# Reordering the seam between the output projection and the feed-forward block of a hybrid encoder layer, on VectorE, ScalarE and GpSimd

## Chip, cores and metric

The kernel runs on one core of one Trainium2 chip. The metric is the device time of one execution in microseconds (us); lower is better. TensorE does the matrix products, VectorE (DVE in the rows), ScalarE (ACT) and GpSimd (POOL) the element-wise work, SyncE (SP) issues the loads.

## The reference, cut to what matters

One layer with D = 1024, 1024 tokens, batch 1, everything in float32. After the mixing part (sliding-window attention beside an mLSTM, outside this change):

```python
mix = jnp.concatenate([rms_norm(att, g_attn_out[l]), rms_norm(mh, g_mlstm_out[l])], axis=-1)
x = x + mix @ w_out[l]
h2 = rms_norm(x, g_ffn[l])
x = x + (jax.nn.silu(h2 @ w_gate[l]) * (h2 @ w_up[l])) @ w_down[l]
```

`w_gate` and `w_up` are 1024 x 2816, `w_down` is 2816 x 1024.

## The kernel before

**Precision and tiles.** Each float32 operand is split into a high part (a copy in a rounded type, made by ScalarE) and a low part (raw minus high, made by VectorE for activations and by GpSimd for weights), and each product is three matmuls: high by high (line 794), high by low (L795 or L796 by the order of operands), low by high. The 1024 tokens are eight tiles of 128 rows, numbered 0 to 7. A transposed activation lies as 128 x 4 x 128 pieces, four k-slices of one tile; four such tiles make a 128 x 2048 array.

**Seven forms.** The feed-forward products use a 2x2 block scheme with seven products in place of eight. The activations are cut into quarters (tiles 0 to 3 or 4 to 7, first or second half of D), the weights of 256 columns likewise, and each of the seven products, called forms and done in the order `FORMS = (1, 2, 6, 5, 7, 3, 4)`, multiplies a quarter or a sum of quarters by a weight quarter or a sum of them. `hf_raw[f]`, `hf_hi[f]` and `hf_lo[f]` are the activation side of form f, `wr_raw`, `wr_hi`, `wr_lo` the weight side. For each activation tile 4 to 7, VectorE's `form_tile` makes four sums at L1640: form 5 from 7 and 4, form 7 from 6 and 7, form 6 from 5 and 6, form 3 from 3 and 6 (each name being the array that holds the operand; the sums overwrite it). For each weight block GpSimd makes four sums (`block_sum`, L724, forms 5, 6, 7, 4) and seven low parts (`block_low`, L730). A sum waits until TensorE has finished with the slot's last use, and until the loads it needs have landed; a low part waits for ScalarE's high copy (`weight_high`, L1288), and that one for the sum.

**Products and their order.** One `half_product` is 12 matmuls of 128 x 512. A block q is one gate or one up block of 256 feed-forward columns, seven products: q = 0 the first gate, q = 1 the first up block, q = 2 the second gate. P1 to P14 are the fourteen products of q = 0 and 1 (`first_gate_up`, L1094), interleaved:

```text
P1 gate form 1     P2 up form 1     P3 gate form 2    P4 up form 2
P5 gate form 6     P6 gate form 5   P7 gate form 7    P8 gate form 3    P9 gate form 4
P10 up form 6      P11 up form 5    P12 up form 7     P13 up form 3     P14 up form 4
```

Products 15 to 21 are the second gate (`gate_up`), product 21 its form 4. Tile 7 is transposed on TensorE (L814) inside P2. The results are combined outside TensorE: ScalarE copies one product from PSUM to `sg[..]` (gate) or `af_raw[..]` (up) with `copy_product`, VectorE adds another one to it with `add_product` (L1968). `sg[1]`, `sg[4]`, `sg[2]` are such partial results of the gate; ScalarE takes the SiLU of them, and VectorE multiplies by the up part (`gated`, L1971). P9 writes into the bank whose earlier content (P7's result) the addition to `sg[4]` reads, so P9 waits for that addition (`added`, second of the block) and for the sixth low part of the activations; product 21 waits for the addition to `sg[4]` of its block in the same way:

```python
pe.wait_ge(added, add_of(0, 1))
pe.wait_ge(h2_flo, 6)
half_product(gate, 0, 4, False)
```

**The seam.** The output projection runs as 16 steps j = 0 to 15, j // 8 choosing the half of the columns, j % 8 the tile. At each step VectorE adds two PSUM banks to the residual x, the first residual addition at L1874 (after `wa_done`) and the second at L1878 (after `wb_done`). From j = 8 on, with tile s = j - 8 then complete, ScalarE takes its statistics (L1472, then `rstd`), VectorE normalises it into `h2buf` (L1660), TensorE transposes it at the next step, ScalarE copies the transposed tile out (`form_tile` of ScalarE), and VectorE makes the sums of a tile two steps behind: tile 4 in step j = 14, tile 5 in j = 15, both after the second residual addition and ahead of the normalisation; tiles 6 and 7 in `dve_first`. After that, VectorE works down a list written by hand (`dve_first`, L2028): the low parts of form 6 (L1652, three quarters, then one), the addition to `sg[1]`, low part 5, the addition to `af_raw[1]`, low parts 7, 3 and 4, one `gated`, the addition to `sg[4]`, and so on. ScalarE's list is `act_first` (L1546), and GpSimd's is the loop over q (L733).

**After P14** VectorE's list goes on with `act_sums` and `dve_gate` of the second gate: `gated` (L1971), four sums (L1982 to 1987), one `act_low` (L1992, the low parts `af_lo` of the up part), one addition, six more `act_low`, and then the addition to `sg[4]` that product 21 waits for. All later gates have the same list. The down block that follows every pair adds PSUM to x on VectorE (L2068).

Of the kernel before, what the change touches and what calls it, by code (L numbers as in the profile page):

```python
# [35 lines left out]
P = 128  # L36
# [38 lines left out]
def hymba_block(nc, x, g_mix, w_in, b_gates, conv_qk, q_gain, k_gain, sinks,  # L75
# [31 lines left out]
    with ctx:  # L107
# [353 lines left out]
        def sum_count(q, f):  # L461

            if q >= QA:
                return 4 * QA + LAST_SUMS.index((q, f)) + 1
            return 4 * q + {5: 1, 6: 2, 7: 3, 4: 4}[f]
# [186 lines left out]
        def _(pool):  # L652
# [80 lines left out]
            for q in range(QA):  # L733
                n = 16 * (q // 2 + 1)
                if q == 1:
# [5 lines left out]
                    block_sum(q, 5, 7, 5)  # L741
                else:
# [5 lines left out]
                pool.wait_ge(wsum, 4 * q + 1)  # L748
                pool.wait_ge(b22_s[q % 2], n)
                block_sum(q, 6, 3, 5)  # L750
                pool.wait_ge(wsum, 4 * q + 2)
                block_sum(q, 7, 3, 7)
                if q == 1:
                    pool.wait_ge(b21_again, 16)
                    block_sum(q, 4, 4, 6)
                else:
# [4 lines left out]
                pool.wait_ge(wsum, 4 * q + 4)  # L761
                for f in FORMS[2:]:
                    block_low(q, f)
# [27 lines left out]
        def _(pe):  # L791
# [302 lines left out]
            def first_gate_up():  # L1094
# [9 lines left out]
                pe.wait_ge(h2_flo, 2)  # L1104
                half_product(gate, 0, 6, False)
                pe.wait_ge(wa_free, 2 * T)
                pe.wait_ge(h2_flo, 3)
                half_product(gate_f, 0, 5, True)
                pe.wait_ge(copied, copy_of(0, 1))
                pe.wait_ge(h2_flo, 4)  # L1110
                half_product(gate, 0, 7, False)
                pe.wait_ge(copied, copy_of(0, 2))
                pe.wait_ge(h2_flo, 5)
                half_product(gate_f, 0, 3, False)
                pe.wait_ge(added, add_of(0, 1))
                pe.wait_ge(h2_flo, 6)
# [107 lines left out]
        def _(act):  # L1224
# [135 lines left out]
            for U in range(ALL):  # L1360
# [105 lines left out]
                if s >= 0:  # L1466
# [79 lines left out]
            def act_first():  # L1546
# [4 lines left out]
                form_high(6, slice(0, 3 * P))  # L1551
# [50 lines left out]
        def _(dve):  # L1602
# [24 lines left out]
            def form_tile(t):  # L1627

                a = slice(t % 4 * P, (t % 4 + 1) * P)
                if t < 4:  # L1630
                    for b in range(2):
                        dve.wait_ge(h2_raw, 2 * t + b + 1)
                        V_.tensor_tensor(hf_lo[1 + b][:, :, a], bank[2 + b][:, :].rearrange("p (k n) -> p k n", k=4),
                                         hf_hi[1 + b][:, :, a].bitcast(F32), ALU.subtract).then_inc(h2_split, 1)
                    return
                dve.wait_ge(h2_raw, 2 * t + 2)
                n = 4 * (t - 4)

# [58 lines left out]
            for U in range(ALL):  # L1697
# [261 lines left out]
                if s >= 6:  # L1959
                    form_tile(s - 2)  # L1960
# [159 lines left out]
```

## Time and profile before

| quantity | value |
|---|---|
| median of 3 runs | 1032.83 us (1032.19 to 1033.6) |
| the profiled execution | 1031.43 us |
| its span | 1029.6 us |
| TensorE matmul busy | 1014.2 us, 99% |
| TensorE weight loads busy | 834.8 us, 81% |
| VectorE busy | 668.5 us, 65% |
| ScalarE busy | 431.9 us, 42% |
| GpSimd busy | 688.9 us, 67% |
| mean granted TensorE clock | 0.997 |
| HBM read, written | 60.48 MB, 4.21 MB |

The profiled execution takes 1.8 us more than its span: that is what lies around the recorded instructions. Its time is 1.40 us under the median of the runs and 0.76 under the quickest of them. Busy shares are means over the whole program; weight loads overlap matmuls. The granted clock is given as a share of full speed, so 1.00 is the 2.4 GHz level. Times within the trace are counted from the start of the span. The step j = 13 of the seam lies at 370 us, P1 starts near 387, P14 ends near 429, and product 21 runs at 446.

### The profile page before, as it was taken

What the parts mean: (1) busy time and instruction counts of PE and PEld (TensorE: products, weight loads), DVE (VectorE), ACT (ScalarE), POOL (GpSimd) and SP (SyncE); (2) the same over time, 40 slices, a digit from 0 to 9 for tenths busy, and PEclk for the clock granted to TensorE, in tenths of its full rate; (3) what the DMA queues carried; (4) which work ended last, traced back from release to release, by engine and by line L of the source; (5) the groups of instructions that cost most, each with busy time, mean ns of one, the idle gap of its engine ahead of it and who ended that gap; (6) DMA issues with size and microseconds to landing.
All of it is one profiled execution on the core that took longest, in us unless ns stands there. A gap on an engine that the chain in (4) does not pass through costs nothing.

```text
span 1029.6 us, 13475 instructions
## 1 busy us (share of the span) xinstructions
PE 1014.2 (99%) x4970; PEld 834.8 (81%) x4970; DVE 668.5 (65%) x790; ACT 431.9 (42%) x895; POOL 688.9 (67%) x543
## 2 busy tenths in 40 slices
PE   9999999999989999999999999999999999999998
PEld 7898778887878887888888888888888888888887
DVE  4259449867772569474857677574857677574585
ACT  7545133347750457533434242433434243433440
POOL 0138668826566514977778688688778688688792
PEclk9999999999999999999999999999999999999999
DMA  7223212140021002111211211211211211211213
GB/s 234 60 62 82 82 33 71 48 147 22 32 104 60 22 21 82 41 52 42 82 41 42 82 42 42 81 41 41 82 42 42 82 41 42 82 41 42 76 62 139
DMA packets 71162, 66.06 MB, mean 64 GB/s; under 512 B 5305, under 2 KB 53689, under 8 KB 71097
## 3 DMA queue, kind: packets, MB, share of 16 engines
q1 hardware_dynamic: 70104, 64.71, 20.3%
q8 instruction: 40, 0.66, 0.3%
q10 hardware_dynamic: 992, 0.49, 0.2%
q14 instruction: 26, 0.20, 0.1%
HBM read 60.48 MB, written 4.21 MB: 63 GB/s over the span
## 4 chain that ended last, share of the span: by engine, by line
PE 75%; DVE 17%; issue 4%; ACT 2%; POOL 1%; DMA 0%; SPq 0%; DVEq 0%; POOLq 0%
PE banks L794 23%; PE banks L796 23%; PE banks L795 23%; DVE af_lo L1992 7%; DVE af_raw L1982 1%; DVE af_raw L1984 1%; ACT prob L1458 1%; PE banks L814 1%; DVE sg L1968 1%; DVE af_raw L1971 1%; PE banks L880 1%; DVE hf_lo L1652 1%; DVE prob L1910 1%; DVE af_raw L1987 1%; DVE smx L1915 1%
## 5 line engine op out<-in xcount | busy, mean ns | idle before, releaser
L730 POOL TENSOR_TENSOR wr_lo<-wr_raw,wr_hi 128x512 fp32r<-128x512 f32 x231 | 316.9, 1401 | 26.9 <-ACT wr_hi L1288 21.8
L724 POOL TENSOR_TENSOR wr_raw<-wr_raw,wr_raw 128x512 f32<-128x512 f32 x132 | 193.0, 1466 | 145.5 <-PE banks L796 113.0
L794 PE MATMUL banks<-hf_hi,wr_hi 128*128 128x512 f32 x616 | 242.4, 394 | 2.8 <-DVE sg L1968 2.0
L796 PE MATMUL banks<-hf_hi,wr_lo 128*128 128x512 f32 x616 | 241.1, 391 | 0.0
L795 PE MATMUL banks<-hf_lo,wr_hi 128*128 128x512 f32 x616 | 240.7, 391 | 0.0
L2068 DVE TENSOR_TENSOR x<-banks,x 128x1024 f32<-128x1024 f32 x138 | 168.8, 1224 | 56.9 <-PE banks L796 43.0
L1288 ACT ACTIVATE wr_hi<-wr_raw 128x512 fp32r<-128x512 f32 x231 | 136.5, 625 | 157.1 <-POOL wr_raw L724 97.6
L794 PE MATMUL banks<-w_hi,actT_hi 128*128 128x512 f32 (+1 forms) x448 | 172.7, 385 | 0.9 <-DVE w_lo L1665 0.9
L796 PE MATMUL banks<-w_hi,actT_lo 128*128 128x512 f32 (+1 forms) x448 | 168.5, 376 | 0.0
L795 PE MATMUL banks<-w_lo,actT_hi 128*128 128x512 f32 (+1 forms) x448 | 168.5, 376 | 0.0
L794 PEld LDWEIGHTS banks<-hf_hi,wr_hi 128*128 128x128 f32 x616 | 116.0, 188 | 31.7 <-DVE sg L1968 6.8
L796 PEld LDWEIGHTS banks<-hf_hi,wr_lo 128*128 128x128 f32 x616 | 115.9, 188 | 25.0
L795 PEld LDWEIGHTS banks<-hf_lo,wr_hi 128*128 128x128 f32 x616 | 116.1, 188 | 24.5
L794 PE MATMUL banks<-wr_hi,af_hi 128*128 128x512 f32 x308 | 120.4, 391 | 0.0
L795 PE MATMUL banks<-wr_lo,af_hi 128*128 128x512 f32 x308 | 120.3, 391 | 0.0
L796 PE MATMUL banks<-wr_hi,af_lo 128*128 128x512 f32 x300 | 117.2, 391 | 0.0
L1968 DVE TENSOR_TENSOR af_raw<-banks,af_raw 128x512 f32<-128x512 f32 x33 | 22.8, 691 | 134.5 <-PE banks L796 134.5
L666 POOL TENSOR_TENSOR w_lo<-w_raw,w_hi 128x512 fp32r<-128x512 f32 (+1 forms) x48 | 61.0, 1271 | 70.5 <-ACT w_raw L1304 67.9
L794 PEld LDWEIGHTS banks<-w_hi,actT_hi 128*128 128x128 f32 x448 | 84.5, 189 | 17.5 <-issue 2.1
L796 PEld LDWEIGHTS banks<-w_hi,actT_lo 128*128 128x128 f32 x448 | 84.6, 189 | 15.7
L795 PEld LDWEIGHTS banks<-w_lo,actT_hi 128*128 128x128 f32 x448 | 84.7, 189 | 13.8
L1992 DVE TENSOR_TENSOR af_lo<-af_raw,af_hi 128x512 fp32r<-128x512 f32 x75 | 90.8, 1263 | 0.3
(202 smaller groups left out, 1210.9 us busy)
## 6 DMA issues: line engine op xcount, KB each, us to landing
wr_raw<-in_w_up SPq DMA_DIRECT2D x46, 256.0 KB, 3.3
wr_raw<-in_w_gate SPq DMA_DIRECT2D x44, 256.0 KB, 3.4
wr_raw<-in_w_down SPq DMA_DIRECT2D x44, 256.0 KB, 3.0
w_raw<-in_w_in SPq DMA_DIRECT2D x32, 256.0 KB, 3.5
w_raw<-in_w_out SPq DMA_DIRECT2D x16, 256.0 KB, 2.6
x<-in_x SPq DMA_DIRECT2D x8, 512.0 KB, 6.4
out<-x SPq DMA_DIRECT2D x16, 256.0 KB, 2.2
x_in<-in_x SPq DMA_DIRECT2D x7, 512.0 KB, 4.4
```

Of the source, the lines that this page charges most:

```text
L666: nc.gpsimd.tensor_tensor(w_lo[:, ring, 0:width], w, w_hi[:, ring, 0:width].bitcast(F32), ALU.subtract).then_inc(w_ready, 1)
L724: nc.gpsimd.tensor_tensor(wr_raw[slot(q, f)][:, :], wr_raw[slot(q, a)][:, :], wr_raw[slot(q, b)][:, :], ALU.subtract).then_inc(wsum, 1)
L730: nc.gpsimd.tensor_tensor(wr_lo[s][:, :], wr_raw[s][:, :], wr_hi[s][:, :].bitcast(F32), ALU.subtract).then_inc(wf_lo, 1)
L794: nc.tensor.matmul(ps, x_hi, wh, start=first, stop=False, skip_group_check=more)
L795: nc.tensor.matmul(ps, x_hi, wl, start=False, stop=False, skip_group_check=more)
L796: return nc.tensor.matmul(ps, x_lo, wh, start=False, stop=last, skip_group_check=more)
L814: last = nc.tensor.transpose(bank[2 + b][:, j * P:(j + 1) * P], src[t % len(src)][:, (4 * b + j) * P:(4 * b + j + 1) * P], ident[:, :])
L880: last = nc.tensor.matmul(bank[6 + i][:, region], scd[:, 2 * pair + i, :], mvx[:, t, 2 * pair + i, :], start=True, stop=t == 0)
L1288: nc.scalar.activation(wr_hi[s][:, :], wr_raw[s][:, :], ACT.Copy).then_inc(wf_hi, 1)
L1968: V_.tensor_tensor(dst[:, :], src[:, :], dst[:, :], ALU.add).then_inc(added, 1)
L1992: V_.tensor_tensor(af_lo[b][f][:, :], af_raw[b][f][:, :], af_hi[b][f][:, :].bitcast(F32), ALU.subtract).then_inc(act_lo_s, 1)
L2068: V_.tensor_tensor(xs, banks[first + h][:, :, :], xs, ALU.add).then_inc(down_add, 1)
```

## The change

Four edits, all between 376 and 425 us of the program:

1. **Sums.** VectorE's `form_tile` for tiles 4 to 7 is cut in two, `first_sums` (forms 5 and 7) and `last_sums` (forms 6 and 3). For tiles 4 and 5 the first two now run between the two residual additions of j = 14 and 15; the last two stay where all four were.
2. **Form 6's first quarter.** The high copy (ScalarE) and the low part (VectorE) of tile 4's quarter of form 6 are made in the seam, the low part in j = 15 between the residual additions; the later instruction covers two quarters in place of three. The counts of `h2_flo` that TensorE waits for go up by one.
3. **`sg[4]`.** ScalarE's copy of P6 to `sg[4]` comes ahead of the SiLU of `sg[1]`, and VectorE's addition to it ahead of low part 4 and of one `gated`.
4. **GpSimd's order for the first up block (q = 1).** Sums 5, 6, 4, low parts 6 and 5, sum 7, low parts 7, 3, 4, in place of sums 5, 6, 7, 4 and low parts 6, 5, 7, 3, 4. The other gate and up blocks keep their order.

The diff, cut to these (the counts of `h2_flo` in `first_gate_up` rise from 2, 3, 4, 5, 6 to 3, 4, 5, 6, 7 in the same way as shown once):

```diff
@@ sum_count
+            if q == 1:
+                return 4 * q + {5: 1, 6: 2, 4: 3, 7: 4}[f]
             return 4 * q + {5: 1, 6: 2, 7: 3, 4: 4}[f]
@@ GpSimd, q == 1
                     block_sum(q, 5, 7, 5)
+                    pool.wait_ge(wsum, sum_count(q, 5))
+                    pool.wait_ge(b22_s[q % 2], n)
+                    block_sum(q, 6, 3, 5)
+                    pool.wait_ge(b21_again, 16)
+                    pool.wait_ge(wsum, sum_count(q, 6))
+                    block_sum(q, 4, 4, 6)
+                    pool.wait_ge(wsum, sum_count(q, 4))
+                    block_low(q, 6)
+                    block_low(q, 5)
+                    block_sum(q, 7, 3, 7)
+                    pool.wait_ge(wsum, sum_count(q, 7))
+                    for f in FORMS[4:]:
+                        block_low(q, f)
...
-                if q == 1:
-                    pool.wait_ge(b21_again, 16)
-                    block_sum(q, 4, 4, 6)
@@ first_gate_up
                 pe.wait_ge(added, add_of(0, 1))
-                pe.wait_ge(h2_flo, 6)
+                pe.wait_ge(h2_flo, 7)
                 half_product(gate, 0, 4, False)
@@ ScalarE, after form_tile(s - 1)
+                    if s == 6:
+                        act.wait_ge(wb_done, T + 5)
+                        act.wait_ge(h2_sum, 3)
+                        form_high(6, slice(0, P))
@@ act_first
-                form_high(6, slice(0, 3 * P))
+                form_high(6, slice(P, 3 * P))
...
                 form_high(4, slice(0, 4 * P))
+                copy_product(sg[4], bank[0], product(0, 5))
                 act.wait_ge(added, add_of(0, 0))
                 silu_of(sg[1], sg[1])
-                copy_product(sg[4], bank[0], product(0, 5))
@@ VectorE
+            def first_sums(t):
+
                 dve.wait_ge(h2_raw, 2 * t + 2)
+                combine(t, 5, 7, 4, ALU.add)
+                combine(t, 7, 6, 7, ALU.subtract)
+
+            def last_sums(t):
+
                 n = 4 * (t - 4)
...
                 dve.wait_ge(h2_sum, n + 2)
+                combine(t, 6, 5, 6, ALU.subtract)
                 dve.wait_ge(h2_sum, n + 3)
+                combine(t, 3, 3, 6, ALU.subtract)
@@ between the residual additions
+                    if j >= T + 6:
+                        first_sums(j - T - 2)
+                    if j == T + 7:
+                        dve.wait_ge(h2_sum, 4)
+                        form_low(6, slice(0, P), 1)
@@ after the second residual addition
                 if s >= 6:
-                    form_tile(s - 2)
+                    last_sums(s - 2)
@@ dve_first
-                form_low(7, slice(0, 4 * P), 4)
-                form_low(3, slice(0, 4 * P), 5)
-                form_low(4, slice(0, 4 * P), 6)
+                form_low(7, slice(0, 4 * P), 5)
+                form_low(3, slice(0, 4 * P), 6)
+                dve.wait_ge(copied, copy_of(0, 2))
+                add_product(sg[4], bank[4], product(0, 7))
+                form_low(4, slice(0, 4 * P), 7)
                 dve.wait_ge(silu_done, 1)
                 dve.wait_ge(added, add_of(1, 0))
                 gated(0, 0, 1, af_raw[0][1])
-                dve.wait_ge(copied, copy_of(0, 2))
-                add_product(sg[4], bank[4], product(0, 7))
```

How the orders on the engines move, at three places (each row is line, operation, output and inputs, shape).

VectorE at j = 15, before. `x_109` is the residual, `hf_raw_149`, `152`, `146`, `155`, `158` are forms 5, 7, 6, 3, 4, `h2buf_114` the normalised tile.

```order
L1874 SCALAR_TENSOR_TENSOR x_109<-banks,rmix,x_109 128x512
L1878 SCALAR_TENSOR_TENSOR x_109<-banks,rmix,x_109 128x512
L1640 TENSOR_TENSOR hf_raw_149<-hf_raw_152,hf_raw_158 128x4x128
L1640 TENSOR_TENSOR hf_raw_152<-hf_raw_146,hf_raw_152 128x4x128
L1640 TENSOR_TENSOR hf_raw_146<-hf_raw_149,hf_raw_146 128x4x128
L1640 TENSOR_TENSOR hf_raw_155<-hf_raw_155,hf_raw_146 128x4x128
L1660 SCALAR_TENSOR_TENSOR h2buf_114<-x_109,rstd,g_row 128x1024
```

and in the change, where `hf_lo_145` is form 6's low part:

```order
L1892 SCALAR_TENSOR_TENSOR x_109<-banks,rmix,x_109 128x512
L1651 TENSOR_TENSOR hf_raw_149<-hf_raw_152,hf_raw_158 128x4x128
L1651 TENSOR_TENSOR hf_raw_152<-hf_raw_146,hf_raw_152 128x4x128
L1670 TENSOR_TENSOR hf_lo_145<-hf_raw_146,hf_hi_144 128x4x128
L1901 SCALAR_TENSOR_TENSOR x_109<-banks,rmix,x_109 128x512
L1651 TENSOR_TENSOR hf_raw_146<-hf_raw_149,hf_raw_146 128x4x128
L1651 TENSOR_TENSOR hf_raw_155<-hf_raw_155,hf_raw_146 128x4x128
L1678 SCALAR_TENSOR_TENSOR h2buf_114<-x_109,rstd,g_row 128x1024
```

Two of the four sums and the new quarter of form 6 now stand ahead of the second residual addition.

VectorE in `dve_first`, behind form 5's low part, before. `hf_lo_151`, `154`, `157` are low parts 7, 3, 4; `sg_254` is `sg[4]`, `sg_252` `sg[1]`, `sg_253` `sg[2]`, `af_raw_212` the up part that is first gated.

```order
L1968 TENSOR_TENSOR af_raw_212<-banks,af_raw_212 128x512
L1652 TENSOR_TENSOR hf_lo_151<-hf_raw_152,hf_hi_150 128x2048
L1652 TENSOR_TENSOR hf_lo_154<-hf_raw_155,hf_hi_153 128x2048
L1652 TENSOR_TENSOR hf_lo_157<-hf_raw_158,hf_hi_156 128x2048
L1971 TENSOR_TENSOR af_raw_212<-af_raw_212,sg_252 128x512
L1968 TENSOR_TENSOR sg_254<-banks,sg_254 128x512
L1968 TENSOR_TENSOR sg_253<-banks,sg_253 128x512
```

and in the change:

```order
L1991 TENSOR_TENSOR af_raw_212<-banks,af_raw_212 128x512
L1670 TENSOR_TENSOR hf_lo_151<-hf_raw_152,hf_hi_150 128x2048
L1670 TENSOR_TENSOR hf_lo_154<-hf_raw_155,hf_hi_153 128x2048
L1991 TENSOR_TENSOR sg_254<-banks,sg_254 128x512
L1670 TENSOR_TENSOR hf_lo_157<-hf_raw_158,hf_hi_156 128x2048
L1994 TENSOR_TENSOR af_raw_212<-af_raw_212,sg_252 128x512
L1991 TENSOR_TENSOR sg_253<-banks,sg_253 128x512
```

The addition to `sg[4]` moved from behind the low part of form 4 and the gated product to ahead of both.

GpSimd in the first up block, before. `wr_raw_161`, `167`, `164`, `176` are the sums of forms 5, 6, 7, 4; `wr_lo_166`, `160`, `163`, `178`, `175` the low parts of forms 6, 5, 7, 3, 4.

```order
L724 TENSOR_TENSOR wr_raw_161<-wr_raw_164,wr_raw_161 128x512
L724 TENSOR_TENSOR wr_raw_167<-wr_raw_179,wr_raw_161 128x512
L724 TENSOR_TENSOR wr_raw_164<-wr_raw_179,wr_raw_164 128x512
L724 TENSOR_TENSOR wr_raw_176<-wr_raw_176,wr_raw_167 128x512
L730 TENSOR_TENSOR wr_lo_166<-wr_raw_167,wr_hi_165 128x512
L730 TENSOR_TENSOR wr_lo_160<-wr_raw_161,wr_hi_159 128x512
L730 TENSOR_TENSOR wr_lo_163<-wr_raw_164,wr_hi_162 128x512
L730 TENSOR_TENSOR wr_lo_178<-wr_raw_179,wr_hi_177 128x512
L730 TENSOR_TENSOR wr_lo_175<-wr_raw_176,wr_hi_174 128x512
```

and in the change:

```order
L726 TENSOR_TENSOR wr_raw_161<-wr_raw_164,wr_raw_161 128x512
L726 TENSOR_TENSOR wr_raw_167<-wr_raw_179,wr_raw_161 128x512
L726 TENSOR_TENSOR wr_raw_176<-wr_raw_176,wr_raw_167 128x512
L732 TENSOR_TENSOR wr_lo_166<-wr_raw_167,wr_hi_165 128x512
L732 TENSOR_TENSOR wr_lo_160<-wr_raw_161,wr_hi_159 128x512
L726 TENSOR_TENSOR wr_raw_164<-wr_raw_179,wr_raw_164 128x512
L732 TENSOR_TENSOR wr_lo_163<-wr_raw_164,wr_hi_162 128x512
L732 TENSOR_TENSOR wr_lo_178<-wr_raw_179,wr_hi_177 128x512
L732 TENSOR_TENSOR wr_lo_175<-wr_raw_176,wr_hi_174 128x512
```

Sum 7 moved behind the low parts of forms 6 and 5.

## Rows read from the trace of the kernel before

**Rows 1.** The page's busy time of each engine.

```profile
PE 1014.2 (99%) x4970; PEld 834.8 (81%) x4970; DVE 668.5 (65%) x790; ACT 431.9 (42%) x895; POOL 688.9 (67%) x543
```

**Rows 2.** List of TensorE's waits: engine, line, releaser, total, times, longest.

```profile
PE banks L794 <- DVE sg L1968: 2.0, 1, 2.0
```

**Rows 3.** TensorE's timeline: start, length, line, instruction, idle before with releaser.

```profile
389.51 0.73 PE L814 MATMUL banks<-ident,h2buf 128*128 128x128 f32 x5
...
402.57 0.39 PE L796 MATMUL banks<-hf_hi,wr_lo 128*128 128x512 f32 x1
403.14 0.47 PE L794 MATMUL banks<-hf_hi,wr_hi 128*128 128x512 f32 x1 [0.18 <-issue]
...
408.48 0.39 PE L796 MATMUL banks<-hf_hi,wr_lo 128*128 128x512 f32 x1
410.87 0.50 PE L794 MATMUL banks<-hf_hi,wr_hi 128*128 128x512 f32 x1 [2.00 <-DVE sg L1968]
...
445.71 0.39 PE L794 MATMUL banks<-hf_hi,wr_hi 128*128 128x512 f32 x1
```

**Rows 4.** TensorE after two earlier gaps, then stretches (PEclk: granted clock).

```profile
233.79 1.16 PE L949 MATMUL banks<-ident,prob 128*128 128x128 f32 x8 [1.94 <-POOL prob L689]
...
304.29 0.87 PE L949 MATMUL banks<-ident,prob 128*128 128x128 f32 x6 [1.88 <-POOL prob L689]
...
234.00:238.00 4.00, 4.00 (x16) 3.35 (x15) 3.86 (x8) 1.18 (x5) 3.05 (x3) 0.59 0.00 0
304.00:308.00 4.00, 3.71 (x33) 3.27 (x34) 1.22 (x3) 2.00 (x5) 3.84 (x5) 1.00 0.00 0
412.00:416.00 4.00, 4.00 (x12) 3.11 (x11) 0.00 (x0) 2.25 (x6) 4.00 (x4) 0.57 0.00 0
416.00:420.00 4.00, 4.00 (x19) 3.21 (x18) 0.00 (x0) 1.55 (x3) 3.92 (x4) 1.00 0.02 4
```

**Rows 5.** VectorE's timeline, the residual additions of j = 13 to 15.

```profile
374.57 1.29 DVE L1660 SCALAR_TENSOR_TENSOR h2buf<-x,rstd,g_row 128x1024 f32<-128x1024 f32 x1 [1.78 <-ACT rstd L1239]
...
378.40 0.75 DVE L1878 SCALAR_TENSOR_TENSOR x<-banks,rmix,x 128x512 f32<-128x512 f32 x1 [1.88 <-PE banks L796]
...
384.75 0.75 DVE L1878 SCALAR_TENSOR_TENSOR x<-banks,rmix,x 128x512 f32<-128x512 f32 x1 [1.08 <-PE banks L796]
...
388.07 1.28 DVE L1660 SCALAR_TENSOR_TENSOR h2buf<-x,rstd,g_row 128x1024 f32<-128x1024 f32 x1
```

**Rows 6.** GpSimd's timeline, seam and second gate.

```profile
376.11 2.54 POOL L730 TENSOR_TENSOR wr_lo<-wr_raw,wr_hi 128x512 fp32r<-128x512 f32 x2 [10.45 <-ACT wr_hi L1288]
...
403.60 7.75 POOL L724 TENSOR_TENSOR wr_raw<-wr_raw,wr_raw 128x512 f32<-128x512 f32 x3 [2.71 <-PE banks L796]
411.43 6.28 POOL L730 TENSOR_TENSOR wr_lo<-wr_raw,wr_hi 128x512 fp32r<-128x512 f32 x5
...
435.08 1.62 POOL L724 TENSOR_TENSOR wr_raw<-wr_raw,wr_raw 128x512 f32<-128x512 f32 x1 [1.42 <-PE banks L796]
...
440.60 4.26 POOL L724 TENSOR_TENSOR wr_raw<-wr_raw,wr_raw 128x512 f32<-128x512 f32 x3 [2.20 <-PE banks L796]
```

**Rows 7.** One line's instructions, 485 to 504 us: shortest, median, longest in ns.

```profile
L1992 DVE TENSOR_TENSOR af_lo<-af_raw,af_hi x7: 681/1772/1786, 493.4 to 500.9; 128x512 fp32r<-128x512 f32 x7
```

**Rows 8.** ScalarE's timeline, the statistics of j = 15.

```profile
385.53 1.06 ACT L1472 ACTIVATE h2buf<-x 128x1024 f32<-128x1024 f32 x1 [3.66 <-DVE x L1878]
```

**Rows 9.** VectorE's timeline, the low parts of forms 7, 3 and 4.

```profile
400.25 8.28 DVE L1652 TENSOR_TENSOR hf_lo<-hf_raw,hf_hi 128x2048 fp32r<-128x2048 f32 x3
```

**Rows 10.** VectorE's timeline, the chain after a block's last product.

```profile
429.34 0.69 DVE L1971 TENSOR_TENSOR af_raw<-banks,sg 128x512 f32<-128x512 f32 x1 [0.27 <-PE banks L796]
...
443.25 0.69 DVE L1968 TENSOR_TENSOR sg<-banks,sg 128x512 f32<-128x512 f32 x1 [0.80 <-PE banks L796]
...
486.92 0.69 DVE L1971 TENSOR_TENSOR af_raw<-banks,sg 128x512 f32<-128x512 f32 x1 [0.55 <-PE banks L796]
...
494.59 8.09 DVE L1992 TENSOR_TENSOR af_lo<-af_raw,af_hi 128x512 fp32r<-128x512 f32 x6
```

More of the change, by code:

```diff
@@ L747, in _ @@
                     block_low(q, 1)
[L748 to L752, printed above, removed]
-                if q == 1:
-                    pool.wait_ge(b21_again, 16)
-                    block_sum(q, 4, 4, 6)
-                else:
+                    pool.wait_ge(wsum, 4 * q + 1)
+                    pool.wait_ge(b22_s[q % 2], n)
+                    block_sum(q, 6, 3, 5)
+                    pool.wait_ge(wsum, 4 * q + 2)
+                    block_sum(q, 7, 3, 7)
                     pool.wait_ge(b21_s[q % 2], n)
@@ L760, in _ @@
                     block_low(q, 2)
-                pool.wait_ge(wsum, 4 * q + 4)
-                for f in FORMS[2:]:
-                    block_low(q, f)
+                    for f in FORMS[2:]:
+                        block_low(q, f)
             for q in (QA, QB):
@@ L1629, in form_tile, with combine @@
                 a = slice(t % 4 * P, (t % 4 + 1) * P)
[L1630 to L1635, printed above, removed]
+                for b in range(2):
+                    dve.wait_ge(h2_raw, 2 * t + b + 1)
+                    V_.tensor_tensor(hf_lo[1 + b][:, :, a], bank[2 + b][:, :].rearrange("p (k n) -> p k n", k=4),
+                                     hf_hi[1 + b][:, :, a].bitcast(F32), ALU.subtract).then_inc(h2_split, 1)
+            def combine(t, f, x, y, op):
+                a = slice(t % 4 * P, (t % 4 + 1) * P)
+                V_.tensor_tensor(hf_raw[f][:, :, a], hf_raw[x][:, :, a], hf_raw[y][:, :, a],
+                                 op).then_inc(h2_sum, 1)
+            def first_sums(t):
                 dve.wait_ge(h2_raw, 2 * t + 2)
+                combine(t, 5, 7, 4, ALU.add)
+                combine(t, 7, 6, 7, ALU.subtract)
+            def last_sums(t):
                 n = 4 * (t - 4)
-                def combine(f, x, y, op):
-                    V_.tensor_tensor(hf_raw[f][:, :, a], hf_raw[x][:, :, a], hf_raw[y][:, :, a],
-                                     op).then_inc(h2_sum, 1)
-                combine(5, 7, 4, ALU.add)
-                combine(7, 6, 7, ALU.subtract)
                 dve.wait_ge(h2_sum, n + 2)
-                combine(6, 5, 6, ALU.subtract)
+                combine(t, 6, 5, 6, ALU.subtract)
                 dve.wait_ge(h2_sum, n + 3)
-                combine(3, 3, 6, ALU.subtract)
+                combine(t, 3, 3, 6, ALU.subtract)
             def form_low(f, a, count):
@@ L2028, in dve_first @@
             def dve_first():
-                form_tile(T - 2)
-                form_tile(T - 1)
+                for t in (T - 2, T - 1):
+                    first_sums(t)
+                    last_sums(t)
                 dve.wait_ge(h2_sum, 12)
-                form_low(6, slice(0, 3 * P), 1)
+                form_low(6, slice(P, 3 * P), 2)
                 dve.wait_ge(h2_sum, 16)
-                form_low(6, slice(3 * P, 4 * P), 2)
+                form_low(6, slice(3 * P, 4 * P), 3)
                 dve.wait_ge(copied, copy_of(0, 0))
                 add_product(sg[1], bank[5], product(0, 2))
-                form_low(5, slice(0, 4 * P), 3)
+                form_low(5, slice(0, 4 * P), 4)
                 dve.wait_ge(copied, copy_of(1, 0))
                 add_product(af_raw[0][1], bank[6], product(1, 2))
-                form_low(7, slice(0, 4 * P), 4)
-                form_low(3, slice(0, 4 * P), 5)
-                form_low(4, slice(0, 4 * P), 6)
+                form_low(7, slice(0, 4 * P), 5)
[3 more added lines that the diff above has]
+                form_low(4, slice(0, 4 * P), 7)
                 dve.wait_ge(silu_done, 1)
```

8 lines of the change are left out of this document (4 added, 4 removed).

## The prediction

> **What bounds the kernel now.** I read four views: busy time, TensorE's waits, the timelines of the four engines at the seam, and the table of stretches with TensorE's clock. TensorE is busy 99% of the span [rows 1], so the end is set by its idle gaps and by its clock. The longest wait for VectorE in the whole program is 2.0 us for the addition to `sg` [rows 2]. Its place is P9, the gate's fourth-form product: the last matmul of P8 starts at 408.48, the next one should follow 0.23 later, but starts at 410.87, so P9 is 2.16 late [rows 3]. P7 starts at 403.14, 0.34 after its turn. After the long gap the clock falls to the lower level: from 412 to 416 us 12 matmuls start, where 19 do in the next 4 us, so seven matmuls of 0.23, **1.6 us**, are lost. The same happened after a gap of 1.94 us ahead of 233.79 (0.59 of full clock); a gap of 1.88 ahead of 304.29 left it at 1.00 in the 4 us that followed [rows 4]. So P9 costs 3.8 us in this execution, and the question is what part of it comes back.
>
> **The seam's sums (j = 14 and 15).** On VectorE the second residual addition of j = 14 starts at 378.40 after 1.88 idle, so the first one ended at 376.52 [rows 5]. Two sums (0.68 each, the next starting 0.08 before the end, so steps of 0.60) fit into that on paper. But GpSimd runs two low parts there, 376.11 to 378.65 [rows 6]. VectorE's instructions with two SBUF inputs and GpSimd's take turns: of seven `af_lo` the quickest took 0.68 and the typical one 1.77 [rows 7], and three sums of GpSimd beside VectorE's low parts took 7.75, where two instructions alone take 2.54 [rows 6]. So the first sum waits to 377.4, the second to 379.1, and the second residual addition starts at 379.6 instead of 378.4. ScalarE's statistics and the normalisation follow it by 1.78 after its end [rows 5]: normalisation at 382.1 (was 381.73). Then addition 383.3, two sums and the early quarter of form 6 (three times 0.60), second addition **385.8 instead of 384.75**, normalisation 388.35 to 389.6 instead of 388.07 to 389.35. TensorE wants it for tile 7's transposes at 389.51 [rows 3]: 0.1 to 0.2 late, a cost of **0.15**. The early quarter on ScalarE costs nothing: it waits there 3.66 us for the addition [rows 8], and without that cover it would be one copy of 0.6.
>
> **From tile 7 to P9.** The chain of sums starts 0.3 later, and form 6's low part is a quarter (0.6) shorter: form 5's low part starts some 0.3 earlier, 397.2. Form 7's low part waits for GpSimd's sum as before and ends at 402.8 (the row at 400.25 less 0.1) [rows 9], so P7 starts at about 402.95 instead of 403.14. Form 3's low part ends at 405.0. Now comes the moved addition to `sg4`: it needs P7, whose result is there 3.0 after its start, at 405.95. VectorE is idle for 0.9 and adds until 406.65. Meanwhile GpSimd, which waited behind form 3's low part for its sum 6, ends that at 406.2, and its next one is now sum 4, whose weights land about 3.3 after P6 (as sum 6 started 3.36 after P5: 403.60 [rows 6], and P5 ends 2.72, twelve matmuls, before P6's 402.96 [rows 3]), at 406.3. It takes the turn 0.3 us ahead of VectorE's form 4, which therefore runs 407.6 to **409.8** (three low parts of 128x2048 took 8.28 with GpSimd's turns, 0.55 and 1.15, in them, so 2.2 each [rows 9]). P8 ends its turn at 408.6, so P9 waits 1.3 and starts at 409.9: **0.95 earlier**. A gap of 1.3 is below the 1.88 that left the clock alone [rows 4], so the 1.6 comes back too. The ScalarE copy of `sg4` moves ahead of the table load and SiLU (1.9 us) and is then 2.5 us early; the next SiLU waits for the addition to `sg4` in any case, so nothing is queued up there. Together TensorE is **2.55 us ahead** by P10: P14 ends at 426.6 instead of 429.2.
>
> **What GpSimd does meanwhile.** Sum 4 to 407.6; low part 6 behind VectorE's form 4, to 411.0; low part 5 behind the gated product, to 412.7; sum 7 to 414.0. ScalarE's high copy of form 7 can only start then (it could at 411.4, right behind the SiLU, before), and behind it stand form 3, two SiLUs, form 4 and the next gate's weights; the copy that P12 needs ends some 4.3 later, 418.3, against P12's turn at 418.2: 0 to 0.2. Low parts 7, 3, 4 (1.25 each): 414.7 to 418.4, where they ended at 417.7 [rows 6]. P10 to P14 get their low parts in time by 1.5 us or more. But GpSimd is now 0.7 later and TensorE 2.55 earlier: **3.2 us of lead are gone**. Before, GpSimd ran its work for the second gate to 433.7 and then was idle 1.42 and again 2.20 until TensorE's products freed slots (435.08 and 440.60) [rows 6]. Both idle times vanish.
>
> **The second gate.** After P14 VectorE works through 11 instructions with two SBUF inputs (four sums and seven `af_lo`) and one addition, and only then makes the addition that product 21 needs. Free of GpSimd that is 0.7 + 11 x 0.60 + 0.6 = 8 us, and each that is blocked adds 1.77 - 0.68 = 1.1 [rows 7]. Now it takes 429.34 to 442.45, 13.1 us, so between four and five are blocked, since GpSimd is idle in part of it; the addition then still waits 0.8 for TensorE [rows 10]. In the gate of j = 2 it takes 15.7 (486.92 to 502.6), seven blocked, four of them in a row in the last six. With GpSimd never idle all eleven are: 20.1. One or two will slip through, since GpSimd still has waits between a sum and the next: I take **19**, nearest to the full one. Starting 426.8 the addition is at 445.8, and product 21 starts at 446.5; TensorE wants it at 443.1 (six products of 2.75 after P14). So there is a **new stall of 3.4 us**, and product 21 starts 0.8 later than the 445.71 of now [rows 3]. The bounds: 15.7 gives no stall (product 21 at 443.3, 2.4 earlier), 20.1 gives 1.9 later. The Trainium skill (SBUF — State Buffer, Who interferes with whom) has the two kinds of instruction exclude each other for their whole length, whichever was issued first; a pair would then take 0.68 + 1.29 = 1.97, the chain of eleven 23, and product 21 would start near 450. The rows show 1.77 for one that had to wait [rows 7], so the sum goes by that.
>
> After a gap of 3.4, longer than both that brought the lower clock, I take another 1.6. **Sum:** +0.8 +1.6 = +2.4 us. Behind it GpSimd catches up in the down block, where VectorE's additions read PSUM and block nobody, and all later gates stay as they are. The profiled execution took 1031.43 (span 1029.6); by it the changed kernel would take 1033.8. The median of the runs is 1.4 higher, about one stretch of lower clock; I add the change to the median: **1035.2 us**. What a measurement of this kernel can tell from no change is 0.2%, 2.07 us.
>
> **Rivals.** A, the forecast: lead of GpSimd lost, stall at product 21, clock lost there: 1035.2. For it: the second gate has only 0.8 us of slack now, and both idle times of GpSimd lie in it. Against: it rests on taking turns eleven times in a row, of which the rows show four [rows 10].
> B, the stall comes but not the lower clock: +0.8, 1033.6. For it: the gap of 1.88 at 304.3 was spared.
> C, the other side: **the gain is kept.** VectorE's chain after P14 stays at the 15.7 of the later gates, because GpSimd finds its slots or ScalarE's copies not ready often enough. It decides at a chain of 18.2: below that product 21 is earlier than now. Price: 2.4 earlier, 1030.4. For it: the gate of j = 2 runs so, and no later wait of TensorE for VectorE is in the list [rows 2]. Against: there GpSimd is idle part of the chain, as four unblocked instructions show, and here it is behind.
> D, VectorE gets form 4 in ahead of sum 4 (0.3 us decide): P9 at 409.0, but product 21 still hangs on the chain after P14, 0.9 earlier with it: +1.5, 1034.3.
> E, all eleven blocked and the transposes or P12 later than I have it: +3.7, 1036.5.
>
> **Numbers.** A 0.42, B 0.20, C 0.18, D 0.10, E 0.10. Slower by over 0.2% (above 1034.9): most of A, E and a little of D, 0.50. Within 0.2%: B, the rest of A and D, a part of C, 0.34. Faster: C, 0.16. The range leaves out C's better part and a tail of E: 1031.4 to 1036.6.
>
> **What would show it.** P9 starting near 409.9 with 1.3 idle before it and a clock of 1.00 at 412 to 416; VectorE idle ahead of the addition to `sg4`; the second residual addition near 379.6; no idle time of GpSimd between 419 and 441; seven `af_lo` of the second gate nearly all at 1.7; a TensorE wait of 3 us for VectorE at product 21, and a stretch of lower clock behind it. I am wrong if product 21 starts before 445, or if P9's gap stays above 1.9.

## The result, and the profile after

The changed kernel takes **1036.55 us** in the median of 6 runs (1035.5 to 1037.41), the kernel before 1032.31 in 6 runs beside it: a ratio of 1.0038 with a 95% interval of 1.0028 to 1.0048 (the medians themselves lie 4.24 us apart). It is slower, as forecast, and the time lies 0.05 us inside the upper end of the stated range. The profiled execution took 1037.41, with a span of 1035.6; its granted clock is 0.997, as before. It is the slowest of its six, and the profiled one of before was quicker than any of its six, so the two traces lie 6.0 us apart where the medians lie 4.2.

From the page, the busy time of each engine, which answers to [rows 1]:

```profile
PE 1014.8 (98%) x4970; PEld 835.1 (81%) x4970; DVE 676.4 (65%) x791; ACT 431.5 (42%) x896; POOL 691.1 (67%) x543
```

TensorE is as busy as before to 0.6 us, and VectorE is 7.9 us busier with one instruction more: nearly all of that is time in which its instructions wait for GpSimd while they count as busy.

The list of TensorE's waits, which answers to [rows 2]:

```profile
PE banks L804 <- DVE sg L1991: 4.5, 2, 3.2
```

One wait of 2.0 for the addition to `sg` has become two, 3.2 and 1.3. TensorE's timeline has them at these places, with P9 (first row) and product 21 (second); the third row is the same product of the sixth gate (j = 5), 234 us later:

```profile
412.05 0.47 PE L804 MATMUL banks<-hf_hi,wr_hi 128*128 128x512 f32 x1 [1.21 <-issue]
...
448.62 0.50 PE L804 MATMUL banks<-hf_hi,wr_hi 128*128 128x512 f32 x1 [3.17 <-DVE sg L1991]
...
682.44 0.50 PE L804 MATMUL banks<-hf_hi,wr_hi 128*128 128x512 f32 x1 [1.30 <-DVE sg L1991]
```

The table of stretches (columns as in [rows 4]: PE, weight loads, VectorE, ScalarE, GpSimd, then the granted clock), behind P9 and behind product 21:

```profile
414.00:418.00 4.00, 4.00 (x19) 3.23 (x18) 0.24 (x1) 1.91 (x4) 3.19 (x3) 1.00 0.00 0
...
450.00:454.00 4.00, 4.00 (x12) 3.18 (x11) 0.00 (x0) 2.13 (x5) 4.00 (x4) 0.60 0.00 0
```

The clock stays at its upper level behind P9, and the lower level with its 12 matmuls in 4 us, seen at 412 before [rows 4], now stands behind product 21.

VectorE's timeline, the split sums of j = 14 and the chain behind P14, which answer to [rows 5] and [rows 10]:

```profile
377.99 0.75 DVE L1892 SCALAR_TENSOR_TENSOR x<-banks,rmix,x 128x512 f32<-128x512 f32 x1
378.65 3.20 DVE L1651 TENSOR_TENSOR hf_raw<-hf_raw,hf_raw 128x512 f32<-128x512 f32 x2
381.77 0.74 DVE L1901 SCALAR_TENSOR_TENSOR x<-banks,rmix,x 128x512 f32<-128x512 f32 x1
...
408.23 0.69 DVE L1991 TENSOR_TENSOR sg<-banks,sg 128x512 f32<-128x512 f32 x1 [1.09 <-PE banks L806]
408.84 3.11 DVE L1670 TENSOR_TENSOR hf_lo<-hf_raw,hf_hi 128x2048 fp32r<-128x2048 f32 x1
...
428.93 0.69 DVE L1994 TENSOR_TENSOR af_raw<-banks,sg 128x512 f32<-128x512 f32 x1 [0.89 <-PE banks L806]
...
436.13 1.67 DVE L2015 TENSOR_TENSOR af_lo<-af_raw,af_hi 128x512 fp32r<-128x512 f32 x1
437.72 0.68 DVE L1991 TENSOR_TENSOR sg<-banks,sg 128x512 f32<-128x512 f32 x1
438.32 9.64 DVE L2015 TENSOR_TENSOR af_lo<-af_raw,af_hi 128x512 fp32r<-128x512 f32 x6
447.89 1.27 DVE L1991 TENSOR_TENSOR sg<-banks,sg 128x512 f32<-128x512 f32 x2
```

The chain from `gated` to the addition that product 21 waits for takes 447.89 - 428.93 = **18.96 us**; it was 13.1 [rows 10], and 19 was forecast. Its seven `af_lo` average 1.67 us. All eleven of its two-input instructions waited for GpSimd, nine in full (1.67 to 1.78) and two in part (1.34 and 1.18). GpSimd's timeline over the same stretch, to hold against [rows 6]:

```profile
423.24 4.26 POOL L726 TENSOR_TENSOR wr_raw<-wr_raw,wr_raw 128x512 f32<-128x512 f32 x3
427.58 9.68 POOL L732 TENSOR_TENSOR wr_lo<-wr_raw,wr_hi 128x512 fp32r<-128x512 f32 x6
437.21 1.75 POOL L726 TENSOR_TENSOR wr_raw<-wr_raw,wr_raw 128x512 f32<-128x512 f32 x1
439.04 1.62 POOL L732 TENSOR_TENSOR wr_lo<-wr_raw,wr_hi 128x512 fp32r<-128x512 f32 x1
440.61 5.14 POOL L726 TENSOR_TENSOR wr_raw<-wr_raw,wr_raw 128x512 f32<-128x512 f32 x3
```

The idle times of 1.42 and 2.20 are gone: each row begins within 0.1 us of the end of the last one.

**Where the time went.** Take the start of each TensorE matmul in the one trace minus its start in the other, instruction by instruction, and read how this difference moves (plus is slower):

| place | change of the difference, us |
|---|---|
| everything up to 389 us | +2.22 |
| tile 7's transposes | +0.20 |
| P7 | -0.40 |
| P9 | -0.83 |
| lower clock of before, behind P9 | -1.56 |
| product 21 | +3.42 |
| lower clock behind product 21 | +1.59 |
| sixth gate | +1.29 |
| all the rest | +0.09 |

The first row is in code that the change does not touch: start-up (1.36 by 9 us) and a stretch of lower clock that lay behind the gap at 232 us before and lies behind the gap at 303 us here. In the eleven profiles below this row is +0.69 to +1.66, so it is mostly the trace of before that was early. The six rows from the transposes to product 21 and its clock sum to **+2.42 us**; the forecast for them was +2.4. With the first row taken off, product 21 starts at 446.40, where 446.5 was forecast. The sixth gate was not forecast.

### The profile page after: what moved, and what is told of

The parts are those of the page before. It is cut to its first block, busy times and chain, and to the rows that moved or that the text cites. A ratio compares the mean times of both kernels' runs of the same rounds, so it can differ in the third digit from the quotient of the medians.

```text
span 1035.6 us, 13449 instructions
## 1 busy us (share of the span) xinstructions
PE 1014.8 (98%) x4970; PEld 835.1 (81%) x4970; DVE 676.4 (65%) x791; ACT 431.5 (42%) x896; POOL 691.1 (67%) x543
## 3 DMA queue, kind: packets, MB, share of 16 engines
q1 hardware_dynamic: 70104, 64.71, 20.1%
## 4 chain that ended last, share of the span: by engine, by line
PE 73%; DVE 18%; issue 4%; ACT 3%; POOL 1%; DMA 1%; SPq 0%; DVEq 0%; POOLq 0%
PE banks L804 23%; PE banks L806 23%; PE banks L805 22%; DVE af_lo L2015 8%; ACT prob L1468 2%; DVE af_raw L2007 2%; DVE af_raw L2005 2%; PE banks L824 1%; DVE sg L1991 1%; DVE af_raw L2010 1%; PE banks L890 1%; DVE prob L1933 1%; DVE smx L1938 1%; DVE af_raw L1994 1%; PE banks L896 1%
## 5 line engine op out<-in xcount | busy, mean ns | idle before, releaser
L732 POOL TENSOR_TENSOR wr_lo<-wr_raw,wr_hi 128x512 fp32r<-128x512 f32 x231 | 321.6, 1421 | 27.8 <-ACT wr_hi L1298 22.7
L726 POOL TENSOR_TENSOR wr_raw<-wr_raw,wr_raw 128x512 f32<-128x512 f32 x132 | 190.5, 1447 | 146.4 <-PE banks L806 111.4
L804 PEld LDWEIGHTS banks<-w_hi,actT_hi 128*128 128x128 f32 x448 | 84.5, 189 | 18.9 <-DVE w_lo L1683 2.3
L2015 DVE TENSOR_TENSOR af_lo<-af_raw,af_hi 128x512 fp32r<-128x512 f32 x75 | 96.1, 1334 | 0.3
```

What stands on the lines that cost most here:

```text
L726: nc.gpsimd.tensor_tensor(wr_raw[slot(q, f)][:, :], wr_raw[slot(q, a)][:, :], wr_raw[slot(q, b)][:, :], ALU.subtract).then_inc(wsum, 1)
L732: nc.gpsimd.tensor_tensor(wr_lo[s][:, :], wr_raw[s][:, :], wr_hi[s][:, :].bitcast(F32), ALU.subtract).then_inc(wf_lo, 1)
L804: nc.tensor.matmul(ps, x_hi, wh, start=first, stop=False, skip_group_check=more)
L2015: V_.tensor_tensor(af_lo[b][f][:, :], af_raw[b][f][:, :], af_hi[b][f][:, :].bitcast(F32), ALU.subtract).then_inc(act_lo_s, 1)
```

## The experiments

Theory: by P10 TensorE is ahead, GpSimd is not, so GpSimd is never idle in the second gate, blocks VectorE's chain, and product 21 waits. First each part of the change alone. The kernel before, measured beside the runs, had a median of 1032.43 us for the first four, 1032.42 for the next four and 1032.08 for the last three; "quicker than the changed kernel" sets a run's median against 1036.55.

**Edits 1 and 2 alone** (the split sums and the early quarter; GpSimd's order, the copy and the addition to `sg[4]` as before).

> The kernel before with the split sums and the early first quarter of form 6 alone (edits 1 and 2); addition to sg[4] and GpSimd's order as before. Theory (GpSimd loses its lead over TensorE at the second gate): TensorE gains only the 0.1 to 0.3 us by which form 5's low part starts earlier, GpSimd keeps both idle times, no wait at product 21; 0.3 us quicker than before, within 0.5 either way. Rival (the sums between the residual additions delay the tiles): most of the 4.2 us of the whole change are here already, the transposes of tile 7 late by over 1 us.

Measured: 1032.22 us in 11 runs against 1032.43 (26 runs), ratio 0.9998 (0.999 to 1.0007). TensorE's difference to before moves by +0.20 at the transposes, -0.41 at P7 and -0.11 at P9. GpSimd keeps both idle times in the second gate (1.47 and 2.24), and product 21 has no gap. The rival falls: these edits cost nothing to be seen.

**Edit 3 alone.**

```diff
                 form_high(4, slice(0, 4 * P))
+                copy_product(sg[4], bank[0], product(0, 5))
                 act.wait_ge(added, add_of(0, 0))
                 silu_of(sg[1], sg[1])
-                copy_product(sg[4], bank[0], product(0, 5))
...
+                dve.wait_ge(copied, copy_of(0, 2))
+                add_product(sg[4], bank[4], product(0, 7))
                 form_low(4, slice(0, 4 * P), 6)
```

> The kernel before with the earlier copy and addition to sg[4] alone (edit 3). Theory: the gap before P9 falls from 2.0 to about 1.2 us, TensorE is then 0.8 us earlier (2.4 with the clock), GpSimd is not, and product 21 waits 2 to 4 us for VectorE; 2 to 3.5 us slower than before. Rival (the moved addition is a gain that something else in the change gives back): 1 to 2.5 us quicker.

Measured: 1034.59 us, ratio 1.0026 (1.0015 to 1.0036), 2.2 slower by the medians, as expected; the rival falls. P9 is 0.86 earlier. The list of TensorE's waits shows the 2.0 gone and this in its place, at product 21:

```profile
PE banks L794 <- DVE sg L1968: 2.5, 1, 2.5
```

The forecast mechanism appears with this edit by itself, GpSimd's order untouched.

**Edit 4 alone** (GpSimd's new order for the first up block).

> The kernel before with GpSimd's new order for the first up block alone (edit 4). Theory: the gap before P9 stays at 2.0; GpSimd ends the up block's work about 0.7 to 2 us later, VectorE's chain after P14 grows, and product 21 waits 1 to 3 us; 1 to 3 us slower. Rival (the order costs nothing, since GpSimd has 3.6 us of idle time in the second gate): within 0.5 of before.

Measured: 1037.34 us, ratio 1.0046 (1.0029 to 1.0063). P9 waits 2.03 as before. Three waits for `sg` in all:

```profile
PE banks L804 <- DVE sg L1978: 6.1, 3, 2.8
```

2.8 is product 21, 1.3 the sixth gate. GpSimd ends its work for the up block 0.75 later against TensorE, as in the whole change; of its idle times 0.68 and 0.50 are left. So a loss of 0.75 is enough: VectorE's chain takes 18.6 with this edit alone, 18.3 with edit 3 alone, which gives away some 2.3 of lead, and 18.96 with both. The losses do not add, since with either one nearly every instruction of the chain already waits. The miss is in size, 4.9 against 1 to 3: behind product 21 comes the lower clock (1.5), and the sixth gate's 1.3. The seven runs lie in two groups, 1033.2 and 1033.5, and five from 1036.9 to 1039.6; which of the gaps the two quick ones do without, their times do not tell.

**The change without edit 4.**

> The changed kernel with GpSimd's order of before (edits 1 to 3). Theory: lead is lost through TensorE's gain at P9 all the same, and the stall at product 21 stays at 3 to 4 us; 2 to 4 us slower than before. Rival (the order alone makes GpSimd late): product 21 no longer waits and the kernel is 2 us quicker than before.

Measured: 1034.41 us, ratio 1.0022 (1.0013 to 1.003). The wait at product 21 is 2.5 instead of 3.2 (3 to 4 were expected), so edit 4 is the last 0.7 of it, the figure that the prediction had for GpSimd's later end. The rival falls. In this profile no lower clock follows the 2.5; it is the quickest of the eleven runs (1033.03), and what the others had there was not traced.

**VectorE's addition two `af_lo` earlier in the second gate**, in the changed kernel:

```diff
+                late = 2 if j == 1 else 0
                 if j >= 1:
-                    for f in FORMS[1:]:
+                    for f in FORMS[1:len(FORMS) - late]:
                         act_low(j - 1, f)
                 dve.wait_ge(copied, 3 * g + 3)
                 add_product(sg[4], bank[4], 7 * g + 5)
+                if j >= 1:
+                    for f in FORMS[len(FORMS) - late:]:
+                        act_low(j - 1, f)
```

> The changed kernel, but in the second gate VectorE makes the addition to sg[4] two af_lo earlier (ahead of forms 3 and 4, which the down block needs last). Theory (product 21 waits only because the addition stands behind a chain that GpSimd blocks): two blocked af_lo are 3.4 us, the stall of 3.2 us and the lower clock behind it go, and product 21 starts within 0.3 of its turn; 4 to 5 us quicker than the changed kernel, about 1031.5, a little less than before. The af_lo of forms 3 and 4 are made 0.6 later and nobody waits. Rival (TensorE is held by something else at that place, and the wait moves to the down block): over 1034.

Measured: 1031.94 us, 4.6 less than the changed kernel; ratio to before 0.9992 (0.9984 to 1.0001). TensorE's difference moves by 0.12 at product 21, instead of 3.42. The rival falls. The wait at product 21 is worth 4.6 us with what follows it. The sixth gate's gap of 1.3 is still there.

**GpSimd held back**, in the changed kernel: ahead of its first sum for the next block it waits for product 19.

```diff
+                    if q == 3:
+                        pool.wait_ge(gu_done, 19)
                     pool.wait_ge(b11_s[q % 2], n)
```

> The changed kernel, but GpSimd starts its work for the down block that follows the second gate (its sum 5) only when product 19 is done, which gives it back an idle stretch in VectorE's chain. Nothing else moves. Theory: from about 437 us on VectorE's remaining af_lo run unblocked, 0.6 each, and the stall at product 21 falls from 3.2 us to under 0.5; 4 to 5 us quicker than the changed kernel, about 1032. Rival (the chain is slow by itself, GpSimd or not): the stall stays at 3 us, no gain, and GpSimd's delay may add to it.

Measured: 1032.12 us, ratio to before 0.9996 (0.9987 to 1.0005), 4.4 less than the changed kernel. VectorE's chain:

```profile
437.51 3.69 DVE L2017 TENSOR_TENSOR af_lo<-af_raw,af_hi 128x512 fp32r<-128x512 f32 x6
441.93 0.69 DVE L1993 TENSOR_TENSOR sg<-banks,sg 128x512 f32<-128x512 f32 x1 [0.73 <-PE banks L808]
```

and GpSimd's timeline, idle meanwhile:

```profile
426.74 9.70 POOL L732 TENSOR_TENSOR wr_lo<-wr_raw,wr_hi 128x512 fp32r<-128x512 f32 x6
441.91 1.30 POOL L726 TENSOR_TENSOR wr_raw<-wr_raw,wr_raw 128x512 f32<-128x512 f32 x1 [5.47 <-PE banks L808]
```

The same six `af_lo` that took 9.64 take 3.69 once GpSimd is idle. VectorE's list is that of the changed kernel, instruction for instruction: GpSimd is what made it slow. Making an engine wait longer made the kernel 4 us quicker. The delay costs 0.4 us elsewhere, a short gap of TensorE in the down block at 450 us, and the gap of 1.3 us that the sixth gate had stands in the eleventh here.

**GpSimd's work doubled at one place**, in the kernel before.

```diff
+                    if q == 1 and f == 4:
+                        s = slot(q, f)
+                        pool.wait_ge(wf_hi, high_count(q, f))
+                        for n_, op in ((1, ALU.subtract), (2, ALU.add)):
+                            nc.gpsimd.tensor_tensor(wr_raw[s][:, :], wr_raw[s][:, :], wr_hi[s][:, :].bitcast(F32),
+                                                    op).then_inc(again, 1)
+                            pool.wait_ge(again, n_)
                     block_low(q, f)
```

> The kernel before, and GpSimd does two more operations of 128x512 in the first up block (form 4's raw weights minus their high copy, plus it again: the value stays), 2.6 us of its time; TensorE's part up to P14 is untouched. Theory: GpSimd comes 2.6 to 3.4 us later to the second gate, its two idle times there go, four more of VectorE's instructions are blocked, and product 21 waits 2 to 3.5 us, with the lower clock behind it: 3 to 5 us slower than before. Rival (only TensorE being earlier makes the stall, GpSimd's 3.6 us of idle time can take this): within 0.5 of before.

Measured: 1036.47 us, ratio 1.0039 (1.0026 to 1.0051). P9 waits 2.01 as before, product 21 waits 3.1 in the list of waits, the lower clock behind it, and the chain takes 18.9. The rival falls. 2.67 us of GpSimd's time, laid where nobody waits for it, cost 4 us thirty microseconds later.

**The addition one `af_lo` earlier in every gate from the second on**, in the kernel before (`late = 1 if j >= 1 else 0` in the diff above).

> The kernel before, and in every gate from the second on VectorE makes the addition to sg[4] one af_lo earlier (ahead of form 4's). Theory: in each of the nine later gates TensorE waits 0.23 us for it now; with the addition up to 1.7 earlier these go, nine times 0.23 is 2.0 us; 1.5 to 2.1 quicker than before. Rival (the 0.23 is what TensorE takes at a wait of any kind): no change.

Measured: 1028.2 us, ratio **0.9956** (0.9944 to 0.9968), twice the gain expected. In the kernel before the first matmul of a later gate's form 4 stands like this in TensorE's timeline:

```profile
502.88 0.39 PE L796 MATMUL banks<-hf_hi,wr_lo 128*128 128x512 f32 x1
503.34 0.50 PE L794 MATMUL banks<-hf_hi,wr_hi 128*128 128x512 f32 x1
503.68 0.40 PE L795 MATMUL banks<-hf_lo,wr_hi 128*128 128x512 f32 x1
```

0.23 late, and then the matmul after it starts 0.34 behind instead of 0.23. The gap of 0.23 costs 0.36 per gate by the difference of the traces, 3.3 us over the nine gates from the third on (the second has no such gap). The remaining 0.9 of the median's gain is not explained: up to P9 this kernel is the one of before, with the same wait of 2.0 and the same chance of the lower clock behind it.

**All together.** The addition two `af_lo` earlier in the second gate and one in the later ones, in the changed kernel, in that without edit 4, and in a kernel before with edit 3's copy and the addition to `sg[4]` behind form 4's low part but ahead of the gated product.

> The changed kernel, with the addition to sg[4] two af_lo earlier in the second gate and one earlier in every later gate. Theory: the second gate's stall goes as when only that gate was edited, and each of the eight later gates gives the 0.36 us per period that the same edit gave the kernel before (57.73 to 57.37): 2.9 us, with the gates' sensitivity to GpSimd's phase (the 1.3 us gap that single gates showed) gone too; about 1028.5, and 0 to 1 us quicker than the kernel before with that edit alone if the 0.8 us at P9 is kept. Rival (edits do not add: the change still costs something behind the second gate): over 1030.

> As the run above, with GpSimd's order of the kernel before. Theory: GpSimd's order matters only by its 0.7 us of lead; with VectorE's addition early enough both orders are within 0.7 us of each other, about 1028.5. Rival (the new order is what lets TensorE keep the gain): this one is over 1 us slower than the run above.

> The kernel before with the smallest edits: the copy to sg[4] early, the addition to it ahead of the gated product but behind form 4's low part, and the addition in the later gates as in the two runs above. Theory: the gap before P9 falls to about 0.5 us (the gated product, 1.7 blocked, no longer stands in front), of which up to 0.7 comes back before P10; 1 to 1.5 us quicker than the kernel before with the later gates' edit alone, about 1027 to 1028. Rival: P10 and product 21 take it back, 1028.5 to 1029.

Measured: 1026.37 us, ratio 0.9946 (0.9934 to 0.9958); 1026.25, 0.9943 (0.9929 to 0.9957); 1027.38, 0.9951 (0.9939 to 0.9964). None has a wait at product 21. The first two agree: GpSimd's order is worth nothing either way once VectorE's addition is early, and both rivals fall. But both are 2 us quicker than the 1028.5 expected. Against the version with the second gate alone, each set against the kernel before beside it, the first gains 5.2 where 2.9 was expected; the traces show 3.3 of it in nine later gates (the expectation counted eight) and 1.2 in the sixth gate's gap, which the expectation named but did not count.

Against the later gates' edit alone, each again set against its kernel before, the first two are 1.5 to 1.6 us quicker. The traces show 1.1 of that (P9 0.9, P7 0.4, less 0.2 at the transposes), and the rest was not taken apart. The third has P9's gap at 0.33, and 0.63 at P10:

```profile
410.02 0.50 PE L794 MATMUL banks<-hf_hi,wr_hi 128*128 128x512 f32 x1 [0.33 <-DVE sg L1968]
...
413.70 0.47 PE L794 MATMUL banks<-hf_hi,wr_hi 128*128 128x512 f32 x1 [0.63 <-POOL wr_lo L730]
```

It is 0.5 to 0.8 us quicker than the later gates' edit alone, less than the 1 to 1.5 expected: part of what P9 gains goes back at P10, as its rival had it, though product 21 takes nothing.

The best version is 5.8 us quicker than the kernel before, and so 10 us quicker than the change.

## Why the prediction was right

**The seam's sums.** Right. The first sum of j = 14 waits behind GpSimd's low parts, 378.65 to 381.85 for both where 1.28 is free of GpSimd; the transposes of tile 7 are 0.20 late (0.15 forecast).

**P9.** Right: forecast 1.3 us late, measured 1.37 (P8's last matmul starts at 410.45, P9 at 412.05, less 0.23), the last step being form 4's low part of 3.11 behind GpSimd's sum 4, as worked out; VectorE is idle for 1.09 ahead of the moved addition (0.9 forecast). The clock behind it is 1.00 as forecast. The reason given for that does not hold. The prediction took the gap of 1.88 that was spared before as a bound for 1.3; in the changed kernel's trace the same place is not spared, and the longer gap 70 us ahead of it is:

```profile
235.21 1.09 PE L959 MATMUL banks<-ident,prob 128*128 128x128 f32 x8 [1.99 <-POOL prob L691]
...
304.94 1.09 PE L959 MATMUL banks<-ident,prob 128*128 128x128 f32 x8 [1.87 <-POOL prob L691]
...
236.00:240.00 4.00, 4.00 (x20) 3.33 (x19) 3.86 (x9) 1.49 (x6) 2.48 (x3) 1.00 0.06 13
306.00:310.00 4.00, 4.00 (x25) 3.23 (x24) 1.25 (x3) 2.07 (x5) 3.72 (x5) 0.57 0.09 32
```

So for gaps near 1.9 us the length does not decide. That a gap of 1.2 is spared is what these traces show, not what the rows of before could tell.

**GpSimd's lead and the second gate.** Right, and this is the step that decides: GpSimd 0.75 later at the end of the up block (0.7 forecast), both idle times gone, the chain at 18.96 (19), the wait at product 21 at 3.2 (3.4), a stretch of lower clock behind it (1.6 forecast, 1.59 measured). The prediction came down from 20.1 to 19 because one or two of the eleven would slip through; none did, but two waited only in part. That GpSimd causes it was an argument before; holding GpSimd back and doubling its work show it from both sides. Rivals B to E fall in the profile, though B's reason is real: one profile of the five with a wait of 2.5 to 3.2 at product 21 had no lower clock. The time is E's, 1036.5, but not E's way: the transposes cost 0.20, P12 nothing, and what lies above the forecast is the sixth gate.

The Trainium skill (SBUF — State Buffer, Who interferes with whom) says that one of the two engines blocks entirely for the other's instruction. The trace agrees that one waits for the other; a chain of 23 us by the sum of both lengths does not come, 18.96 does. A full step of VectorE's chain is 1.70 with GpSimd busy throughout, not 1.97.

**What was mis-sized.** The term for P9's lower clock, -1.6, holds in the pair of traces, where before had it. In the median it is smaller: of five profiles with a wait of 1.9 to 2.1 us at P9 (before, edits 1 and 2 alone, edit 4 alone, the doubled work, the later gates' edit in before) two have the lower clock behind it, three have not. A change cannot get back what most runs do not lose. That the six rows of the traces sum to +2.42, so near the forecast, is therefore partly luck: it takes a trace of before with the lower clock behind P9 and one of the change with it behind product 21.

**"All later gates stay as they are" failed.** That is the other part of why 4.2 us came and not 2.4. The sixth gate lost 1.29. GpSimd's timeline ahead of it, in the changed kernel:

```profile
656.76 2.65 POOL L726 TENSOR_TENSOR wr_raw<-wr_raw,wr_raw 128x512 f32<-128x512 f32 x2
659.75 1.29 POOL L726 TENSOR_TENSOR wr_raw<-wr_raw,wr_raw 128x512 f32<-128x512 f32 x1 [0.33 <-issue]
661.12 9.69 POOL L732 TENSOR_TENSOR wr_lo<-wr_raw,wr_hi 128x512 fp32r<-128x512 f32 x6
```

A pause of 0.33 for nothing that the profile shows shifts the turns, eight of VectorE's instructions are blocked instead of seven, the chain takes 16.92 instead of 15.67, and the addition comes 1.3 too late. In the gate before it, the three sums run without the pause and the chain is as ever. All five profiles of kernels with edit 4 have one such pause in a gate (0.31 to 0.33), four of them with a gap of 1.3 there; the remaining one is the version whose later additions are early, and it has none. In four of the five the pause stands ahead of the same instruction of GpSimd, whatever the time; in the one where GpSimd is held back, which has one wait more in its list, it stands 165 instructions further on. The eight profiles with GpSimd's old order show no such pause behind the start of the program. Why the new order brings it stays open, and that the pause causes the gap is argued from their standing together: no run took the pause away alone. The forecast could have held a term for something of this kind by seeing how little slack the later gates have: 0.23 us late already, every one.

**The medians.** The version with only the second gate mended is 0.5 under its kernel before, and its profile has the sixth gate's loss in it, 1.2. If that loss is in most runs, which is taken for granted here, the gain up to P10 is 1.7 in the medians, where the prediction's terms had 2.55, with 1.6 of it for a lower clock that most runs do not lose. Against it stand 4.6 for the wait at product 21 with its clock (3.4 and 1.6 forecast) and 1.2 for the sixth gate (nothing forecast). That these parts add up to about 4.2 is no check on them, since two of them are differences of the same medians.

The mechanism is what the prediction said. That the time falls within its range is luck: the change is 1.8 us larger than forecast, and the range was laid around a median of three runs before, 1032.83. With the 1032.31 of the six runs beside the change, the same range would have ended at 1036.1.

## What to carry to other kernels

When an edit makes the bounding engine earlier, ask which other engine does not get earlier with it: its idle time was the slack, and if it shares a resource with a third engine, the loss shows up where that third engine's list is longest, one block later. Look for the result that the bounding engine waits for and move it ahead of work that is needed later; that was worth more than any change of who works when, and it also took away the sensitivity to small shifts. A wait that repeats in every block, however short, is the first thing to look at: nine gaps of 0.23 us paid more (3.3) than the one gap of 2 us (0.9 in the traces).

## What the runs showed of the hardware that was not expected

A gap of 0.23 us ahead of one matmul costs TensorE 0.36, since the next start is 0.34 behind instead of 0.23. VectorE's six two-input instructions of 128x512 take 9.64 us beside a busy GpSimd and 3.69 beside an idle one; the chain of eleven takes 18.3 to 19.0 in all five kernels in which product 21 waits, by whatever edit GpSimd came late. The same wait of 2.0 us on TensorE is followed by the lower clock in some executions and not in others, so one profile's clock is no term for a median. And in the kernels with edit 4, GpSimd pauses for 0.3 us, with no releaser in the profile, ahead of one instruction, the same in four of five.
